# MLP up projection: two products in one 512-column pass, the third added by VectorE, low parts one tile later

## The reference, cut to what matters

```python
def squared_relu_mlp(h, w1, w2):
    return jnp.square(jax.nn.relu(h @ w1)) @ w2
```

## Time and profile before

| | before |
|---|---|
| median of 3 runs | 1038.48 us (1035.58 to 1039.99) |
| span of the profiled execution, first to last instruction | 1034.6 us |
| around the span (the median less it) | 3.9 us |
| PE busy | 967.8 us (94%) |
| DVE busy | 722.6 us (70%) |
| ACT busy | 545.4 us (53%) |
| granted TensorE clock, mean | 0.986 |

### The profile page before, as it was taken

One profiled execution on the slowest core, in us unless ns is written; L12 is line 12 of the kernel. 1 busy time (PEld: TensorE's weight loads), 2 busy tenths in 40 slices (PEclk: granted clock), 3 DMA queues, 4 the chain that ended last, 5 costly groups with the idle time before them and its releaser, 6 DMA issues.

```text
span 1034.6 us, 14650 instructions
## 1 busy us (share of the span) xinstructions
PE 967.8 (94%) x5676; PEld 781.8 (76%) x5676; DVE 722.6 (70%) x1113; ACT 545.4 (53%) x873; POOL 50.9 (5%) x39
## 2 busy tenths in 40 slices
PE   6886988999999999999899999989999999998995
PEld 3663657989888867777798989877888887875684
DVE  3488657876878787667885644578555778797775
ACT  3357733654445353655455445435556656657662
POOL 0000001500000000000250100000000000000000
PEclk9999999999999999999999999999999999999998
DMA  9747465979898577432688865654434256541041
GB/s 350 264 143 295 164 244 183 292 267 330 305 311 295 196 279 268 132 113 83 227 287 234 242 203 177 202 163 162 148 106 154 95 165 194 188 163 62 31 164 41
DMA packets 106931, 204.85 MB, mean 198 GB/s; under 512 B 3488, under 2 KB 37680, under 8 KB 106864
## 3 DMA queue, kind: packets, MB, share of 16 engines
q1 hardware_dynamic: 103808, 193.26, 55.4%
q0 software_dynamic: 3056, 10.67, 3.5%
HBM read 202.76 MB, written 1.15 MB: 197 GB/s over the span
## 4 chain that ended last, share of the span: by engine, by line
PE 66%; DVE 17%; ACT 6%; DMA 6%; issue 3%; SPq 1%; ACTq 0%; DVEq 0%
PE bank L1702 13%; PE bank L1704 13%; PE bank L1703 13%; DVE w_lo L1881 5%; PE bank L1756 5%; PE bank L1758 4%; PE bank L1757 4%; DMA raw<-in_mlp_w 3%; PE bank L1777 3%; ACT w_hi L1309 2%; PE bank L1799 2%; DMA raw<-in_ab_w_in 2%; PE bank L1595 1%; DMA raw<-in_ada_w 1%; PE bank L1829 1%
## 5 line engine op out<-in xcount | busy, mean ns | idle before, releaser
L1881 DVE TENSOR_TENSOR w_lo<-raw,w_hi 128x2048 fp32r<-128x2048 f32 (+2 forms) x134 | 309.7, 2320 | 145.7 <-ACT w_hi L1309 144.7
L1309 ACT ACTIVATE w_hi<-raw 128x2048 fp32r<-128x2048 f32 (+2 forms) x134 | 248.6, 1858 | 132.9 <-PE bank L1704 64.7
L1702 PE MATMUL bank<-w_lo,ht_hi 128*128 128x512 f32 (+1 forms) x544 | 217.4, 400 | 11.9 <-DVE w_lo L1881 6.3
L1704 PE MATMUL bank<-w_hi,ht_lo 128*128 128x512 f32 (+1 forms) x528 | 205.5, 389 | 0.0
L1703 PE MATMUL bank<-w_hi,ht_hi 128*128 128x512 f32 (+1 forms) x528 | 205.2, 389 | 0.0
L1702 PEld LDWEIGHTS bank<-w_lo,ht_hi 128*128 128x128 f32 x544 | 102.9, 189 | 41.6 <-issue 19.6
L1756 PE MATMUL bank<-ht_hi,w_lo 128*128 128x256 f32 x448 | 127.6, 285 | 2.2 <-DVE w_lo L1881 2.2
L1757 PE MATMUL bank<-ht_lo,w_hi 128*128 128x256 f32 x448 | 126.8, 283 | 0.0
L1758 PE MATMUL bank<-ht_hi,w_hi 128*128 128x256 f32 x448 | 126.7, 283 | 0.0
L1704 PEld LDWEIGHTS bank<-w_hi,ht_lo 128*128 128x128 f32 x528 | 100.0, 189 | 21.3
L1703 PEld LDWEIGHTS bank<-w_hi,ht_hi 128*128 128x128 f32 x528 | 100.2, 190 | 18.6
(11 more groups left out here) (250 smaller groups left out, 1324.9 us busy)
## 6 DMA issues: line engine op xcount, KB each, us to landing
raw<-in_mlp_w SPq DMA_DIRECT2D x64, 1024.0 KB, 6.5
raw<-in_ada_w SPq DMA_DIRECT2D x44, 1024.0 KB, 5.3
raw<-in_a_w_in SPq DMA_DIRECT2D x16, 1024.0 KB, 5.3
raw<-in_c_w_in SPq DMA_DIRECT2D x12, 1024.0 KB, 6.4
raw<-in_b_w_in SPq DMA_DIRECT2D x10, 1024.0 KB, 5.1
raw<-in_ple_w_gate SPq DMA_DIRECT2D x8, 1024.0 KB, 5.0
raw<-in_ab_w_in SPq DMA_DIRECT2D x4, 1024.0 KB, 10.0
tok<-in_ada_w SPq DMA_DIRECT2D x4, 1024.0 KB, 12.8
```

The lines of the kernel that those rows point to most:

```text
L1309: nc.scalar.activation(split_parts(n)[0], raw_tile(t), ACT.Copy).then_inc(high_done, 1)
L1702: nc.tensor.matmul(dst, a_hi[:, c, rows], lo[:, k, :], start=it["first"] and k == 0, stop=False)
L1704: mm = nc.tensor.matmul(dst, a_lo[:, c, rows], hi[:, k, :], start=False, stop=it["last"] and k == it["kc"] - 1)
L1881: nc.vector.tensor_tensor(lo, raw_tile(split[n]), hi.bitcast(F32), ALU.subtract).then_inc(low_done, 1)
```

## The change

The high and the low activations are laid out in one buffer `ht`, so that for one contraction step they are 512 moving columns. High weights meet both in one matmul: one half of the bank collects high x high, the other high x low. Low weights meet the high activations in a second matmul of 256 columns, in the first half. So a tile has 2 x 8 x 2 = 32 matmuls in place of 48, and takes two banks in place of one; the pairs (0, 1) and (2, 3) take turns, and the second tile of up 0 has (4, 5).

The two bank halves have to be added. ScalarE copies the second half of each bank to SBUF, VectorE adds the first half to it (`hidden_sum`), and ScalarE then waits for both sums before Relu, Square and the high part, all now from SBUF. The low part of the rows of a tile moves in VectorE's program from behind its own tile to behind the `split_low` of the next (`hidden_low`).

```diff
         def up(g, ada=(), copied=None):
+            held = None
             for j in range(2):
                 if copied and j == 0:
                     continue
-                bk = banks()
                 for h in range(2):
                     c0 = g * 1024 + j * 512 + h * 256
+                    bk = banks((4, 5) if copied and h else None)
                     n = tile(w1[:, :, c0:c0 + 256], KD, 256, "split")
-                    it = add("hidden", tile=n, half=h, banks=bk, cut=cuts["ht"], buf=g % 2, c0=4 * j)
...
+                    add("hidden", tile=n, banks=bk, cut=cuts["ht"])
+                    hidden_low(held)
+                    slot = 2 * j + h
+                    held = add("hidden_sum", tile=n, banks=bk, slot=slot, buf=g % 2, c0=4 * j + 2 * h, high=tick("high"), cross=tick("cross", 2),
+                               emptied=cut_of.get(slot, 0))
...
+            hidden_low(held)
             hid_cut[g] = count["cut"]
@@ ScalarE
+                elif kind == "hidden_sum":
+                    both = full[:, it["slot"], :]
+                    act.wait_ge(tile_done, it["tile"] + 1)
+                    if it["emptied"]:
+                        act.wait_ge(split_done, it["emptied"])
+                    for c, (b, _) in enumerate(it["banks"]):
+                        nc.scalar.activation(both[:, c * S:(c + 1) * S], bank[b][:, S:2 * S], ACT.Copy).then_inc(cross_copied, 1)
+                    b, used = it["banks"][1]
+                    act.wait_ge(bank_free[b], used + 1)
+                    link(nc.scalar.activation(both, both, ACT.Relu))
+                    link(nc.scalar.activation(both, both, ACT.Square))
+                    nc.scalar.activation(hid_hi[:, it["buf"], it["c0"]:it["c0"] + 2, :], both.rearrange("p (c s) -> p c s", c=2),
+                                         ACT.Copy).then_inc(high_copied, 1)
@@ TensorE
-                            nc.tensor.matmul(dst, lo[:, k, cols], ht_hi[:, k, :], start=k == 0, stop=False)
-                            nc.tensor.matmul(dst, hi[:, k, cols], ht_lo[:, k, :], start=False, stop=False)
-                            mm = nc.tensor.matmul(dst, hi[:, k, cols], ht_hi[:, k, :], start=False, stop=k == KD - 1)
+                            if k < KD - 1:
+                                nc.tensor.matmul(bank[b][:, :], hi[:, k, cols], ht[:, :, k, :], start=k == 0, stop=False)
+                            nc.tensor.matmul(bank[b][:, 0:S], lo[:, k, cols], ht_hi[:, k, :], start=False, stop=False)
+                        mm = nc.tensor.matmul(bank[b][:, :], hi[:, KD - 1, cols], ht[:, :, KD - 1, :], start=False, stop=True)
                     mm.then_inc(tile_done, 1)
@@ VectorE
+                elif kind == "hidden_sum":
+                    for c, (b, used) in enumerate(it["banks"]):
+                        part = full[:, it["slot"], c * S:(c + 1) * S]
+                        dve.wait_ge(cross_copied, it["cross"] - 1 + c)
+                        nc.vector.tensor_tensor(part, bank[b][:, 0:S], part, ALU.add).then_inc(bank_free[b], 1)
+                        dve.wait_ge(bank_free[b], used + 1)
+
+                elif kind == "hidden_low":
+                    c0 = it["c0"]
+                    dve.wait_ge(high_copied, it["high"])
+                    low_part(hid_lo[:, it["buf"], c0:c0 + 2, :], full[:, it["slot"], :].rearrange("p (c s) -> p c s", c=2),
+                             hid_hi[:, it["buf"], c0:c0 + 2, :])
```

More of the change, by code:

```diff
@@ L128, in make_plan @@
     plan, tiles = [], []
-    count = {"split": 0, "ada": 0, "sums": 0, "product": 0, "job": 0, "rows": 0, "cut": 0, "pair": 0, "index": 0, "gated": 0, "ssq": 0, "high": 0, "x": 0, "half": 0}
+    count = {"split": 0, "ada": 0, "sums": 0, "product": 0, "job": 0, "rows": 0, "cut": 0, "pair": 0, "index": 0, "gated": 0, "ssq": 0, "high": 0, "x": 0, "half": 0, "cross": 0}
     cuts = {}
@@ L412, in entered, with hidden_low @@
             return [(b, used + 1) for b, used in bk]
+        def hidden_low(it):
+            if it:
+                add("hidden_low", slot=it["slot"], buf=it["buf"], c0=it["c0"], high=it["high"])
+                cut_of[it["slot"]] = tick("cut")
         def up(g, ada=(), copied=None):
+            held = None
             for j in range(2):
@@ L972, in block_kernel @@
         u = sb("u", [P, T, D])
-        ht_hi = sb("ht_hi", [P, KD, S], F32R)
-        ht_lo = sb("ht_lo", [P, KD, S], F32R)
+        ht = sb("ht", [P, 2, KD, S], F32R)
+        ht_hi, ht_lo = ht[:, 0, :, :], ht[:, 1, :, :]
         plt_hi = sb("plt_hi", [P, 2, S], F32R)
@@ L1068, in block_kernel @@
         high_copied = sem("high_copied")
+        cross_copied = sem("cross_copied")
         split_done = sem("split_done")
@@ L1418, in _ @@
                     elif end == "hidden":
[L1419 to L1425, removed]
+                        b, used = it["banks"][0]
+                        c0 = it["c0"]
+                        act.wait_ge(job_done, it["job"])
                         if it["emptied"]:
@@ L1744, in _ @@
                     n = it["tile"]
-                    b, used = it["banks"][it["half"]]
-                    enter([(b, used)])
                     pe.wait_ge(split_done, it["cut"][0])
@@ L1749, in _ @@
                     hi, lo = views(n)
-                    for c in range(2):
-                        dst = bank[b][:, c * S:(c + 1) * S]
+                    for c, (b, used) in enumerate(it["banks"]):
+                        enter([(b, used)])
                         for k in range(KD):
@@ L2113, in _ @@
                         continue
[L2114 to L2120, removed]
+                    if end == "hidden":
                         b, used = it["banks"][1]
```

## The result

| | before | after |
|---|---|---|
| median, us (lowest to highest) | 1038.41 (1035.58 to 1039.99) | 1073.68 (1070.24 to 1076.72) |
| executions | 4 | 4 |
| ratio of the times, 95% interval | | 1.0341 (1.0319 to 1.0364) |
| span of the profiled execution | 1034.6 | 1074.7 |

The change makes the kernel 35.3 us slower. (Before is the median of four executions here, of three in the table ahead of the prediction, which is why it was 1038.48 there.) The forecast was 1071.5 us, within 1053 to 1086. The profiled execution of after is the longest of its four (spans of the others 1071.2, 1070.5 and 1068.4), so the difference of the two profiles, 40.1 us, is some 5 us larger than that of the medians.

What follows compares the result with a forecast made beforehand. TensorE was taken as the bound (PE busy 94% of a 1034.6 us span). Layer 0's 23 us and layer 1's 10 sum to 33: a span of 1067.6, a median of 1071.5 us, range 1053 to 1086.

Steps and rivals of the forecast that it cites:

- The loop: Hidden tiles: each turn goes round ScalarE and VectorE once, 7.53 us a tile against TensorE's 5.55.
- Layer 1: Layer 1's MLP: +6.2 us by up 2, +1.8 for each of up 2 and up 3; taken as +10.
- Tiles D, E, F: Last three of the first six hidden tiles A to F, either layer: TensorE starts them at 19.8, 25.7, 33.3 us.
- G: First of the down tiles G to J behind the first six hidden tiles: starts at 44.1 us.
- The wait ahead of `gate_row`: Behind tile F, TensorE stands 3.4 us until additions(E) free bank pair (0, 1).
- Layer 0: Layer 0's MLP: the loop, plus weight loads no longer hidden by a lead of two tiles; +23 us.
- The step through `sum_rows`: Layer 0, behind tile 36: needs additions(35) at 344.6, so tile 37 starts at 345.6, against 321.7 before.
- TensorE's term: Hidden tiles: one 0.227 us matmul replaces a 0.240 pair, 0.21 us less a tile, 5.9 over 28 tiles.
- Additions beside POOL: First additions while POOL works: up to 2.3 us later each layer if they suffer; none taken, 5 us in the range.
- layer 0 absorbs its share: Rival: loads get ahead while TensorE waits, so layer 0 costs what layer 1 does; +20, 1058.5 us; chance 0.18.
- the lead gives nothing: Rival: all 28 tiles pay 1.8 us, +50, 1088 us; chance 0.10.
- the loop is hidden: Rival: the loop is under 5.55 us, so only TensorE's 5.9 us gain remains, 1032.6 us; chance 0.05.

Runs made afterwards that it cites:

- e1: The changed kernel with VectorE's w_lo(n+2) moved behind the two additions of tile n instead of ahead of them; 1043.05 us.
- e5: The changed kernel with ScalarE's w_hi(n+3) moved between the two copies of tile n and the wait for its additions; 1037.48 us.
- e2: The changed kernel with the low part of a tile's rows directly behind its own additions on VectorE, not one tile later; 1072.28 us.
- e8: The changed kernel with two more VectorE multiplications of 128x256, results unused, ahead of the additions; 1104.54 us.
- e4: The changed kernel's wide matmuls without copies or additions, Relu reading the banks' first halves and high x low left out of the result; 1034.37 us.
- e9: The changed kernel with both moves: w_hi(n+3) ahead of ScalarE's wait for the additions, and w_lo(n+2) behind the additions on VectorE; 1040.97 us.

## Why the prediction was right

**The loop: shown.** Forecast 7.53 us, measured 7.59; the difference is w_hi to w_lo, 2.00 where rows of before had 1.93. e1 and e5 open it from either side and bring layer 1 to TensorE's rate, e2 takes a term out and e8 puts one in, each by its size to within 0.1 us.

**Layer 1: +10 forecast, +10.3 measured.** Tiles D, E, F at 20.1, 25.9, 33.5 (19.8, 25.7, 33.3), G at 42.9 (44.1), up 2 at 67.0 (67.5). The wait ahead of `gate_row` was 2.1 us and not 3.4. Each of up 2 and up 3 then took 2.3 more than before, not 1.8, mostly because TensorE's tile gained less. So two small errors, 0.5 at the start and twice 0.5 behind it, nearly cancel. That F agrees is luck: w_lo(F) was done 0.9 us earlier than forecast (32.4), and TensorE then waited another 1.1 for a bank, until D's additions were done.

**Layer 0: +23 forecast, +25.9 measured.** From the first hidden matmul, tile 28 was at 98.3 (97.0 forecast), 32 at 125.9 (124.6), 36 at 153.2 (152.2), 37 at 162.7 (162.2). (The forecast's start of tile 22, 240.1, should be 240.0 by its own terms, 183.35 + 56.6.) The step through `sum_rows`, which waits for a bank that the additions free, was there: 2.7 us. At tile 37 the kernel was 24.3 us behind the one before (23.9 forecast; the sum took 23). Another 1.6 came within that tile. TensorE's granted clock fell to its lower level, 1.2 GHz (columns of this view: stretch, its length, busy time and count by engine, granted clock, DMA share, GB/s):

```profile
348.00:350.00 2.00, 2.00 (x7) 1.53 (x6) 1.93 (x3) 1.97 (x3) 0.00 (x0) 0.50 0.00 0
350.00:352.00 2.00, 2.00 (x8) 1.58 (x7) 1.55 (x2) 1.26 (x3) 0.00 (x0) 0.67 0.57 117
```

That followed the 2.7 us wait for the bank and 16 matmuls with 32 columns of weights. The clock column (0.50 lost in 2 us, 0.33 in the next 2) makes it about 1.7 us. I had no term for it, and it was not tested by itself. The profile of after has two more such times, in tile 26 of layer 0 (behind a wait of 2.3 us; the tile takes 7.0 us) and in tile 20 of layer 1 (behind the wait ahead of `gate_row`; 7.3 us in place of 5.6). They cost next to nothing, because what follows waited for the loop: tile 27 starts 7.6 us after tile 26, a turn, and tile 22 starts at 56.0 in layer 1 and at 56.2 in layer 0, whose tile 20 ran at the full clock.

**TensorE's term was mis-sized.** Wide matmuls were to come at 0.227, the rate of a row of wide ones alone. Next to narrow ones a pair takes 0.353, so the wide one costs 0.23 to 0.24, and a tile gains 0.11 to 0.13, not 0.21. Over 28 tiles that is 3 to 3.6 us and not 5.9. (e4's median is 3.4 below that of before, but that it is the same figure is luck: its stretches gave 6.1 and the rest of the execution took some back.) The Trainium skill ("TensorE: Matmul & The Clock Gate", section "Back-to-back issue gap") gives an isolated matmul about 2.5 ns beyond its columns, by which I had estimated a gain of 1 us. The measured gain lies between that and mine: rows of one kind cost 13 to 14 ns beyond their columns here, and a pair in turn 33 for the two. The loop hid most of the error.

**Additions beside POOL: right.** Those of layer 0's tile A ran while POOL worked and took 0.42 each (418 ns by their group); the operation on two SBUF operands right behind took 1.26 for 512 columns, where a low part of the same size takes 0.68 (timelines of DVE and POOL):

```profile
193.54 0.87 DVE L2179 TENSOR_TENSOR full<-bank,full 128x256 f32<-128x256 f32 x2
...
195.17 1.26 DVE L2138 TENSOR_TENSOR full<-full 128x512 f32<-128x512 f32 x1
...
191.54 4.33 POOL L1282 TENSOR_TENSOR x<-x,b_row 128x1024 f32<-128x1024 f32 x1
```

**Left out.** While the loop runs, TensorE waits for w_lo and then again, shorter, for its banks: pair by pair they are freed by additions that stand behind w_lo. The view of the waits has 7.0 us in layer 0 that end with an addition and not with w_lo (tile F: w_lo done at 32.4, the bank free and TensorE started 1.1 us later). Most of that is time in which TensorE would have waited for w_lo anyway, and the down tiles behind a group don't need these banks; so I take the cost beyond what was counted as small. No run separates it.

**Rivals.** That layer 0 absorbs its share (1058.5) fell: it paid 25.9 and layer 1 10.3. ScalarE waited less for loads, as forecast (46.9 us, from 56.7), but it spent the time waiting for VectorE instead. That the lead gives nothing (1088) fell too, since down groups win it back: in layer 1 the four tiles from the start of up 2 (67.0, 72.6, 78.3, 83.9 us) follow each other without a wait. That the loop is hidden (1032.6) fell with the 7.59; e5 opens the loop by an edit that the change did not have, and even it comes to 1037.5, since TensorE gained less and layer 0 gave 0.4 us in all.

**The rest.** Outside the two MLP stretches the profiled executions differ by 3.9 us, which I did not trace. The stretches give 36.2, the medians 35.3. The same rest is 1.4 in e5 and 3.8 in e1, whose work outside is the same, so part of it varies by execution. But it is above nothing in all eleven changed kernels, 0.6 to 4.0 us against the one profile of before, so a small cost of the change outside the MLP is not excluded. That the median came within 2.2 us of the forecast is in part luck: the mis-sized gain, the clock and this rest added time, and the shorter wait ahead of `gate_row` took some off.

## What to carry to other kernels

When an edit makes engine A wait for engine B's work on the same tile, write down both queues in program order and add up one turn through both: what is prepared ahead for later tiles stands in it, and idle time on either engine does not help (7.59 us a tile with both engines under 5 us of work). Moving one prepared step past the wait on one engine opens the loop at no cost in work, but which engine matters where loads are tight: here it was better to leave w_lo, which TensorE and the next loads wait for, where it was (e5 1037.5 us, e1 1043.1). And measure the gain without the new cost first: here it was 0.3% of the time. When stretches of two profiles are compared, look at the granted clock in each before the difference is put down to the edit.

## What the runs showed of the hardware that was not expected

- A 512-column matmul between 256-column ones costs more than in a row of its own kind: a pair takes 0.353 us, where the rows of either kind alone give 0.227 + 0.120 = 0.347. The 6 ns are small, but a tile has 16 pairs, and that is 0.1 us of the 0.21 hoped for.
- Beside POOL's work on SBUF, VectorE's operations on two SBUF operands stretch (0.42 to 2.62 us for 128x256 in e8, 0.69 to 1.26 for 128x512 in after), while the additions of one PSUM and one SBUF operand kept their 0.42 us. Each stretched one ended 0.3 to 0.6 us behind the POOL operation beside it (193.94 and 193.65 in e8, 196.43 and 195.87 in after, 194.86 and 194.31 in before), as if it had been held until then.
- TensorE's granted clock went to 1.2 GHz for 3.4 us with waits of TensorE of 1.8 to 4.5 us, in the MLP stretches of seven of the eleven changed kernels (three times in after, nine in e8, one of them twice as long) and never in those of before. Not every such wait had it: one of 3.1 us in e8 did not. Where TensorE is the bound this adds up to 1.7 us to what the wait costs (tile 37 in after, tile 26 in e1 and e9); where it isn't, it adds nothing.
